# Three tiles of an out-projection instead of two beside the last unit of an attention, the third in a PSUM bank that a linear attention has left

## The reference, cut to what matters

```python
y_a = dilated_attention(heads(aq, A_HEADS), heads(ak, A_HEADS), heads(av, A_HEADS), bias_a)
y_b = gla(heads(bq, B_HEADS), heads(bk, B_HEADS), heads(bv, B_HEADS), br, ba, w_a2, b_a, gla_norm_w)
y_c = moba_attention(heads(cq, C_HEADS), heads(ck, C_HEADS), heads(cv, C_HEADS), bias_c)
mix = jnp.concatenate([y_a.reshape(Bsz, S, A_WIDTH), y_b, y_c.reshape(Bsz, S, C_WIDTH)], axis=-1)
x = x + mix @ w_out

h2 = rmsnorm(x, norm2_w)
x = x + jnp.square(jax.nn.relu(h2 @ w_ff1)) @ w_ff2
```

## Time and profile before

| what | us |
|---|---|
| median of 3 runs | 2373.51 |
| lowest and highest | 2368.49, 2374.42 |
| the profiled execution, its span | 2372.1 |
| PE busy in it | 2274.8 (96%) |
| DVE, ACT, POOL busy | 1418.8, 903.4, 512.3 |
| first attention's last unit and out-projection, from the first wait for part 0 to the end of tile 3 | 284.9 to 323.1 from the span's start |

### The profile page before, as it was taken

One profiled execution on the slowest core, in us unless ns is written; L12 is line 12 of the kernel. 1 busy time (PEld: TensorE's weight loads), 2 busy tenths in 40 slices (PEclk: granted clock), 3 DMA queues, 4 the chain that ended last, 5 costly groups with the idle time before them and its releaser, 6 DMA issues.

```text
span 2372.1 us, 30169 instructions
## 1 busy us (share of the span) xinstructions
PE 2274.8 (96%) x11614; PEld 1881.8 (79%) x11614; DVE 1418.8 (60%) x2334; ACT 903.4 (38%) x1521; POOL 512.3 (22%) x363
## 2 busy tenths in 40 slices
PE   7989799999999999989999999999899999999998
PEld 5655588888887875669999999999676568888887
DVE  5475657889857457774675565544736776434335
ACT  4244533232343224882522222122422794423232
POOL 2332123232221211001312121111121002322221
PEclk9999899999999999999999999999999999999999
DMA  4211016555421321001243343421122002223321
GB/s 165 89 63 55 27 36 241 205 186 186 160 93 38 118 82 59 27 19 36 96 134 129 122 133 121 140 96 58 56 98 96 32 28 80 98 89 100 105 89 54
DMA packets 76250, 227.71 MB, mean 96 GB/s; under 512 B 9151, under 2 KB 12608, under 8 KB 76108
## 3 DMA queue, kind: packets, MB, share of 16 engines
q1 hardware_dynamic: 70928, 216.69, 27.1%
q0 software_dynamic: 1856, 6.07, 0.7%
q10 hardware_dynamic: 3324, 3.02, 0.4%
HBM read 220.99 MB, written 4.76 MB: 95 GB/s over the span
## 4 chain that ended last, share of the span: by engine, by line
PE 84%; DVE 8%; ACT 4%; issue 2%; POOL 1%; ACTq 0%; DMA 0%; DVEq 0%; SPq 0%; POOLq 0%
PE psum L765 31%; PE psum L1083 24%; PE psum L839 3%; PE psum L1461 3%; PE psum L786 3%; PE psum L734 3%; PE psum L1492 2%; PE psum L859 2%; PE psum L1343 1%; PE psum L1415 1%; PE psum L1476 1%; PE psum L1107 1%; PE psum L671 1%; PE psum L1302 1%; PE psum L1428 1%
## 5 line engine op out<-in xcount | busy, mean ns | idle before, releaser
L765 PE MATMUL psum<-mix_split,weight_split 128*128 128x384 f32 (+1 forms) x3072 | 620.6, 363 | 2.0 <-DVE weight_split L1565 2.0
L765 PEld LDWEIGHTS psum<-mix_split,weight_split 128*128 128x128 f32 x3072 | 555.5, 188 | 62.9 <-DVE weight_split L1565 2.5
L1083 PE MATMUL psum<-hidden,weight_split 128*128 128x512 f32 (+1 forms) x2880 | 584.5, 364 | 0.0
L1083 PEld LDWEIGHTS psum<-hidden,weight_split 128*128 128x128 f32 x2880 | 521.5, 188 | 59.7
L2486 ACT CAST weight_split<-weight_ring 128x1024 fp32r<-128x1024 f32 x269 | 277.4, 1041 | 286.6 <-PE psum L1083 221.1
L3117 POOL TENSOR_TENSOR weight_split<-weight_ring,weight_split 128x1024 fp32r<-128x1024 f32 x89 | 231.2, 2598 | 496.1 <-ACT weight_split L2486 495.9
L1981 DVE TENSOR_TENSOR hidden<-hidden_tmp,hidden 128x512 fp32r<-128x512 f32 (+1 forms) x98 | 138.5, 1416 | 313.2 <-POOL hidden_tmp L3259 313.2
L3259 POOL TENSOR_TENSOR hidden_tmp<-hidden_tmp 128x512 f32<-128x512 f32 (+1 forms) x98 | 125.3, 1279 | 592.0 <-ACT hidden L2789 591.8
L1565 DVE TENSOR_TENSOR weight_split<-weight_ring,weight_split 128x1024 fp32r<-128x1024 f32 x180 | 226.6, 1260 | 40.1 <-ACT weight_split L2486 40.1
L2783 ACT ACTIVATE hidden_tmp<-psum 128x512 f32<-128x512 f32 (+1 forms) x94 | 62.7, 667 | 467.3 <-PE psum L765 467.0
L2004 DVE SCALAR_TENSOR_TENSOR residual<-psum,modulation,residual 128x512 f32<-128x512 f32 (+3 forms) x232 | 117.7, 552 | 135.2 <-PE psum L1083 134.9
(11 more groups left out here) (343 smaller groups left out, 2917.3 us busy)
## 6 DMA issues: line engine op xcount, KB each, us to landing
weight_ring<-in_w_mlp SPq DMA_DIRECT2D x128, 512.0 KB, 3.9
weight_ring<-in_w_ff SPq DMA_DIRECT2D x64, 512.0 KB, 4.7
mod_ring<-in_w_mod SPq DMA_DIRECT2D x48, 512.0 KB, 3.8
late_ring<-in_w_mod SPq DMA_DIRECT2D x96, 256.0 KB, 3.7
weight_ring<-in_w_in SPq DMA_DIRECT2D x45, 512.0 KB, 3.7
weight_ring<-in_w_out SPq DMA_DIRECT2D x24, 512.0 KB, 3.6
weight_ring<-in_tables SPq DMA_DIRECT2D x13, 512.0 KB, 3.7
weight_ring<-in_w_v SPq DMA_DIRECT2D x8, 512.0 KB, 3.9
```

Of the source, the lines that this page charges most:

```text
L765: m = pe.matmul(psum[:, b + r, 0:hi - lo], w[:, part_w, :], moving(x, part_x, k, lo, hi), start=k == 0 and part_w + part_x == 0, stop=k == ...
L1083: mm = pe.matmul(psum[:, b + r, 0:hi - lo], w[:, part_w, :], G[:, part_x, f % (2 * GROUP), lo:hi], start=jj == 0 and part_w + part_x == 0, ...
```

## The change

The generator runs three tiles: m = 0, 1, 2 in banks 6, 7 and 2. Bank 2 is one of the linear attention's two. Each step of the loop over parts has nine matmuls in place of six. Tile 2 is no longer made as a product of its own, so `take(2)` is called once less, and every bank that `take` gives later in the program is two further back than it was. Load 27 (the weights of tile 2) is rounded by ACT and split by DVE within the attention, at places of their own at the start of the last unit. In the second block, only the banks change.

```diff
-        OUT_ORDER, OUT_CUTS = [0, 1, 2, 5, 6, 3, 4, 7], (2, 4, 6, 7)
+        OUT_ORDER, OUT_CUTS, OUT_FIRST = [0, 1, 2, 5, 6, 3, 4, 7], (2, 4, 6, 7), 3
+
+        def together(tag):
+
+            n = OUT_FIRST if tag == "out1" else 2
+            return [tuple(range(n))] + [(i,) for i in range(n, PARTED)]
...
-            def out_pair():
-
-                at = [use_load("w_out1", m, split=True) for m in range(2)]
+            def out_three():
+
+                at = [use_load("w_out1", m, split=True) for m in range(OUT_FIRST)]
                 for n, k in enumerate(OUT_ORDER):
                     if n in OUT_CUTS:
                         yield
                     for m, load in enumerate(at):
                         j = split_at[load]
-                        b = bank_of["out1", m] = 6 + m
+                        b = bank_of["out1", m] = (6, 7, 2)[m]
                         if n == 0:
                             pe.wait_ge(*when(lo_of(j), j))
                             wait_bank(b)
...
-                for i in range(2, PARTED):
+                for i in range(OUT_FIRST, PARTED):
                     product("out1", [(i, ("w_out1", i))], HS_T1, X1, None, lambda i, r: ("out1_vec", ("add", i, r)))
...
                 for u in range(NH):
+                    if u == NH - 1:
+                        split_lo(load_at["w_out1", OUT_FIRST - 1])
                     for n in range(4 * u, 4 * u + 4):
...
                     if filler(u) is not None:
                         stage("w_in1", filler(u))
+                    else:
+                        split_hi(load_at["w_out1", OUT_FIRST - 1])
                     for n in range(4 * u, 4 * u + 4):
```

More of the change, by code:

```diff
@@ L1028, in mixers @@
                 pools["gemm"], pools["turn"] = [6], [3, 4, 5]
-                out = out_pair()
+                out = out_three()
                 for u in range(NH):
@@ L1954, in out_tiles @@
             def out_tiles(tag, name, ranges, norm_tag, gate):
-                for ms in [(0, 1)] + [(i,) for i in range(2, PARTED)]:
+                for ms in together(tag):
                     for m in ms:
@@ L2757, in out_tiles @@
             def out_tiles(tag, name, ranges, norm_tag):
-                for ms in [(0, 1)] + [(i,) for i in range(2, PARTED)]:
+                for ms in together(tag):
                     for m in ms:
                         split_hi(two_on(name, m))
-                    if ms == (2,):
+                    if ms == together(tag)[1]:
                         root_table(norm_tag)
```

## The result

| | median, us | executions | against before |
|---|---|---|---|
| before | 2373.66 (2368.49 to 2376.78) | 12 | |
| after | 2377.81 (2375.18 to 2381.46) | 12 | ratio 1.0024, 95% interval 1.0016 to 1.0031 |

The changed kernel is slower by about 0.24% by the ratio, that is 5.7 us, between 3.8 and 7.4 by the interval; the two medians lie 4.15 us apart. The forecast was 2378.2 us and 4.7 us more than before. The profiled execution of the changed kernel has a span of 2377.5 us, 5.4 above the 2372.1 of before. The same code stands 5 to 9 lines lower than in before: L997 is now L1002, L1565 is L1570, L1966 is L1973, L3202 is L3211.

What follows compares the result with a forecast made beforehand. The prediction took PE's own queue to bound the kernel (84% of the chain of waits). Its terms, 3.3 us for load 27 and 1.4 for the bank, made 2373.5 + 4.7 = 2378.2 us, range 2371.5 to 2383.5.

Steps and rivals of the forecast that it cites:

- The wait for load 27: Ahead of tile 2's first matmul in the first attention's last unit: PE waits for DVE's split, going on 3.3 us later.
- The bank's 1.4 us: Layer 1, second block: tile 2 gets tile 1's bank and waits for DVE's addition, 1.4 us later.
- item 47's late scaling: Last unit: ACT's scaling at 296.9 in place of 294.60, behind DVE's later reciprocal; costed at zero.
- the later weights: Behind the last unit: the next tiles' weights are not late, loads 28 and 29 being cast in time; costed at zero.
- a difference of zero: Last unit, behind the wait: 5.2 us at 1.2 GHz as before, so no clock cost; range -0.9 to 0.8 us.
- rival 2: Last unit: slower by the clock, 3.4 us more in all, 8.1 in sum, 2381.6 us; chance 0.14.
- the second half of rival 2: Ahead of part 7: the clock falls at the 2.68 us gap for 3.4 us, costing another 1.7 us.
- Rival 2's first half: Behind the wait for load 27: full clock returns one stretch of 3.4 us later, costing 1.7 us more.
- the sign by which rival 2 was to be recognized: Last unit: PEclk still 0.50 more than 6 us behind the wait, or 0.50 in part 7's matmuls.
- Rival 1: Last unit: DVE goes ahead of POOL, split ends at 295.6; sum 3.7 us, 2377.2 us; chance 0.18.
- Rival 3: Last unit: load 27's split is in time, the 1.42 us gap filled, clock back sooner; -1.7 us, 2371.8; chance 0.08.

Runs made afterwards that it cites:

- e1_banks_back: The changed kernel with one more take(2) behind tile 3, so later banks are those of the kernel before: 2376.49 us, ratio 1.0016.
- e6b_split_first: The changed kernel with DVE's split of load 27 moved between the gate's reciprocal and the rest of part 2: 2376.30 us, ratio 1.0013.
- e3_bank_alone: The kernel before with tile 2 of layer 1's out-projection given the bank of tile 1: 2374.53 us, ratio 1.0003.
- e2_early_split: The changed kernel with load 27 cast and split earlier, in idle time of ACT and DVE: 2370.34 us, ratio 0.999.
- e4_both: The changed kernel with load 27 cast and split earlier and the banks of before: 2366.89 us, ratio 0.998; run again, 2369.15 us, ratio 0.9987.
- e5b_split_alone: The kernel before with load 27 cast and split at the early places of e2_early_split: 2374.30 us, ratio 1.0003.
- e8b_three_ahead: e4_both with tile 3's first seven parts run between the last values and part 7 of tiles 0 to 2: 2371.33 us, ratio 0.9991.
- e10_rest_late: e4_both with parts 1 to 6 of tile 2 run behind the last values product, ahead of part 7: 2368.02 us, ratio 0.9979.

## Why the prediction was right, and where it wasn't

**Terms of the sum.** The wait for load 27 was put at 3.3 us and is 3.31. Its chain held link by link: ACT's cast ahead of DVE's split (forecast for 292.6 to 293.6; it ran from 292.82 to 293.86), DVE's split behind the reciprocal and the rest of part 2, POOL's multiplication first, a split of about 2.3 us from issue (2.28). The bank's 1.4 us, with bounds of 1.3 and 1.6, is 1.53 between the rows' starts, and 1.37 as idle time. That all else costs nothing held for item 47's late scaling (ACT waited 3.29 us for it, and PE never for ACT) and for the later weights: no row ahead of tiles 3 to 7 shows an idle time ended by `weight_split`. The point of the forecast, 2378.2, lies 0.4 us from the measured median.

**What it had wrong** is the clock, "a difference of zero". The first half of it held: behind the wait PE had 1.2 GHz for some 5 us, as before. But in after's profile part 7 was at 1.2 GHz as well and took 3.85 us for nine matmuls, where the full clock gives 2.33. That is the second half of rival 2, priced at 1.7 us; it measures 1.5. Rival 2's first half, a clock that comes back one stretch later, didn't happen.

Is it an effect of the change? That isn't shown. Of the profiles with the gap of 2.68 us left open, the three in which PE had waited 3 us or more for load 27 had the low clock behind it (after, e1_banks_back and e6b_split_first: 3.85, 3.77 and 3.66 us). But so had e3_bank_alone, whose last unit is that of before: it lost 0.3 us in part 7 and 1.4 in the 48 matmuls behind. In the other five (before, e2_early_split, both of e4_both, e5b_split_alone) the clock was full. Three of three against one of six leaves it open, each being a single execution. Nor do the mean granted clocks bear it out. A further 3.4 us at 1.2 GHz in every execution would by estimate lower a kernel's mean by 0.0007 (half of 3.4 us in 2377), but the means are 0.9866 for after, 0.9868 for e1_banks_back and 0.9871 for e6b_split_first, against 0.9869 for before (each known to some 0.0002, e1_banks_back's to 0.0005). So the sign by which rival 2 was to be recognized, a low clock in the matmuls of part 7, can't decide for it: it can appear without its cause.

**Why the total came out all the same.** By the rows the two places cost 3.3 + 1.5 us, and part 7's clock 1.5 more, 6.3 in all. The profile's span gives 5.4, since the clock that was low in part 7 was high in the first MLP, where before had it low. These two nearly cancel, 1.5 against 1.55, so between these two executions the clock came to about nothing, as forecast, but in two places and by chance. The two terms of the sum, measured at 3.31 and 1.53, make 4.8; the ratio gives 5.7 (3.8 to 7.4), and the medians 4.15. So the terms and their mechanism are right, and the hit of 0.4 us on the median is closer than these runs can tell: that much is luck.

**The rivals.** Rival 1 is out by the row of 2.28 us. e6b_split_first shows what the turn on DVE and POOL is worth, together with that of the rest of part 2, which it puts behind the split: 3.06 us of idle time in place of 4.72, so 1.66 less, where rival 1 alone had 1.05. Rival 3 didn't come about by the change as it stands, but e2_early_split is what it described: the split is there in time. I had given it -1.7 us with the bank's 1.4 in; measured are -2.4 (-4.3 to -0.2). The mechanism was right and the size agrees, and all that was missing in the change was an earlier place for one cast on ACT and one split on DVE.

## What to carry to other kernels

Work that fills an idle time of the bound engine brings its own inputs with it. Look for the last of them in the other engines' queues before you look at the gap: here 5.4 us of matmuls were moved to fill 1.42 us, and one split behind a 3.34 us reciprocal turned that into 4.72. The place of that cast and that split was worth some 8 us by the ratios, more than the whole idea.

Fill a gap with work whose buffers are free and whose early end nobody needs, such as the rest of a tile that is already under way or the next tile, as long as the ring behind it still has a slot: e8b_three_ahead and e10_rest_late move nearly the same matmuls, and only the second shows no new idle time behind them. And where banks or buffers are dealt out by one counter for the whole program, a call less at one place is a wait at another: put the counter back, or follow it to the end.

## What the runs showed of the hardware that I had not expected

The same idle time with the same work directly ahead of it lowers the granted clock in one execution and not in another. PE's 2.68 us ahead of part 7 left it at 1.00 in five profiles. In three others it went with 0.55 to 0.58 over the 3.4 to 3.6 us behind it, and in a fourth, e3_bank_alone, with 0.50 from 1.2 us behind the gap on, though the code of that unit is the same as in before. The 2.04 us in the first MLP did so in before and not in after. Each time it costs some 1.5 to 1.7 us, as much as the edits compared here. A low clock that is found in a single profile is therefore not yet the edit's doing.

PE kept busy by small matmuls through its idle times had the full clock from 292 to the end of the unit, and saved 4.1 us of the last unit by the profile, though only 1.7 to 3.3 us of the time.
